# Expert stage of a decoder step: every U group in three passes, with top-k and routing spread over the groups, and the modulated norms in four parts

## The reference, cut to what matters

```python
sh1, sc1, gt1, sh2, sc2, gt2 = split(c @ w_ada + b_ada, 6)
h  = rmsnorm(x, norm1_w) * (1 + sc1) + sh1          # first modulated norm
proj = h @ w_in                                     # attention and delta-rule branches follow
x  = x + gt1 * (mixed @ w_out)
h2 = rmsnorm(x, norm2_w) * (1 + sc2) + sh2          # second modulated norm
qh = h2 @ w_peer_q                                  # 8 heads x 256
s1, s2 = qh[..., :128] . keys[:, 0], qh[..., 128:] . keys[:, 1]    # 8 heads x 2 x 128 scores
v1, i1 = top_k(s1, 16); v2, i2 = top_k(s2, 16)
best, sel = top_k(v1[:, None] + v2[None], 16)       # 16 of 256 pairs a head
wts = softmax(best); eidx = i1 * 128 + i2 at sel    # 128 experts a token, of 16384
act = gelu(h2 . w_peer_u[eidx])
y = x + gt2 * sum(wts * act * w_peer_v[eidx])
```

## Time and profile before

| | |
|---|---|
| median of three runs | 3261.43 us (3259.88 to 3264.95) |
| the profiled execution's own time | 3260.47 us |
| its span, first to last instruction | 3258.7 us |
| PE, PEld busy | 92%, 84% of the span |
| DVE, ACT, Pool busy | 51%, 28%, 23% |
| granted PE clock, mean | 0.952 |

### The profile page before, as it was taken

The page is one execution under the profiler, slowest core; times in us unless marked ns, Lnnn a source line. Parts: engine busy times, 40 slices in busy tenths (PEclk is TensorE's granted clock), DMA queues, the critical chain, the costliest instruction groups (busy, mean ns, idle before and its releaser), DMA issues.

```text
span 3258.7 us, 51780 instructions
## 1 busy us (share of the span) xinstructions
PE 3001.6 (92%) x20823; PEld 2725.9 (84%) x20823; DVE 1676.7 (51%) x2590; ACT 921.3 (28%) x1187; POOL 749.9 (23%) x269
## 2 busy tenths in 40 slices
PE   5799999877787997997999999999999999999999
PEld 2588877556684886997888889999999999999999
DVE  0348616535315003823297765444445776767675
ACT  1011002412111211333201554333333343434341
POOL 0000000000000002442100004544444454545452
PEclk8899999887876998998999999999999999999999
DMA  9577766371203666552444436555555666566663
GB/s 399 230 268 254 252 248 208 96 247 52 84 33 135 246 249 273 208 182 107 168 146 174 160 159 232 205 205 205 204 205 207 234 220 233 220 229 224 222 232 130
DMA packets 144309, 650.46 MB, mean 200 GB/s; under 512 B 22470, under 2 KB 84294, under 8 KB 103110
## 3 DMA queue, kind: packets, MB, share of 16 engines
q1 hardware_dynamic: 134550, 614.26, 50.9%
q10 hardware_dynamic: 9648, 34.61, 2.7%
HBM read 605.12 MB, written 52.07 MB: 202 GB/s over the span
## 4 chain that ended last, share of the span: by engine, by line
PE 82%; DVE 8%; DMA 5%; ACT 2%; issue 1%; SPq 1%; DVEq 1%; ACTq 0%
PE psum L978 16%; PE psum L979 16%; PE psum L980 15%; PE psum L557 15%; PE psum L1060 7%; DMA ring<-in_w_ada 3%; PE psum L537 2%; PE psum L768 1%; PE psum L1087 1%; PE psum L847 1%; PE psum L932 1%; PE psum L949 1%; DVE arena L1704 1%; DMA route_w<-arena 1%; DVE arena L2055 1%
## 5 line engine op out<-in xcount | busy, mean ns | idle before, releaser
L557 PE MATMUL psum<-hT,ring 128*128 128x264 f32 x2560 | 590.6, 393 | 12.6 <-DVE xT L1845 6.6
L979 PE MATMUL psum<-act_hi,w_lo 128*128 128x264 f32 x2048 | 584.9, 286 | 0.0
L557 PEld LDWEIGHTS psum<-hT,ring 128*128 128x128 f32 x2560 | 491.6, 193 | 106.4 <-issue 15.2
L978 PE MATMUL psum<-act_hi,part 128*128 128x264 f32 x1920 | 546.9, 285 | 2.8 <-DVE hT L2124 2.8
L980 PE MATMUL psum<-act_lo,part 128*128 128x264 f32 x1920 | 547.3, 285 | 0.0
L499 POOL TENSOR_TENSOR w_lo<-ring,wd_hi 128x1024 fp32r<-128x1024 f32 x48 | 129.5, 2717 | 1446.9 <-ACT wd_hi L1417 1446.9
L516 POOL TENSOR_TENSOR w_lo<-ring,part 128x1024 fp32r<-128x1024 f32 x112 | 311.7, 2790 | 387.3 <-ACT part L1543 386.0
L979 PE MATMUL psum<-h_hi,w_lo 128*128 128x264 f32 x1376 | 390.3, 284 | 0.0
L979 PEld LDWEIGHTS psum<-act_hi,w_lo 128*128 128x128 f32 x2048 | 386.0, 188 | 0.0
L978 PE MATMUL psum<-h_hi,part 128*128 128x264 f32 x1288 | 366.2, 284 | 2.5 <-issue 2.5
L980 PE MATMUL psum<-h_lo,part 128*128 128x264 f32 x1288 | 365.5, 284 | 0.0
(11 more groups left out here) (421 smaller groups left out, 4592.7 us busy)
## 6 DMA issues: line engine op xcount, KB each, us to landing
ring<-in_w_peer_u SPq DMA_DIRECT2D x64, 2048.0 KB, 8.1
ring<-in_w_peer_v SPq DMA_DIRECT2D x128, 1024.0 KB, 6.9
ring<-in_w_ada SPq DMA_DIRECT2D x48, 2048.0 KB, 11.2
ring<-in_w_in SPq DMA_DIRECT2D x42, 2048.0 KB, 7.9
gelu_scratch<-CK ACTq DMA_DIRECT2D x64, 264.0 KB, 7.8
route_w<-arena ACTq DMA_DIRECT2D x3, 5632.0 KB, 17.6
Wb<-route_w SPq DMA_DIRECT2D x96, 176.0 KB, 3.8
ring<-in_cache_cmp SPq DMA_DIRECT2D x64, 256.0 KB, 4.8
```

The costliest lines, as they stand in the source:

```text
L557: mm = pe.matmul(bank[b + j][:, 0:NT], w[:, k, j * P:(j + 1) * P], hT[:, k, :], start=(k == 0), stop=(k == KT - 1))
L978: pe.matmul(out, w_top, x_top, start=start, stop=False)
L979: pe.matmul(out, w, x_top, start=False, stop=False)
```

## The change

1. The w_ada loads no longer wait for the constants, and come in the order scale, scale, shift, shift (`FIRST_ADA`), so that every four tiles complete four of the 16 feature tiles. PE sums the squares of x before the w_ada loop; ACT's root and DVE's inverse and product with it follow there. `modulate` is cut into four parts of four feature tiles, each run by DVE after its four w_ada tiles, and PE's small product waits part by part.
2. The second norm is cut in the same way; ACT's hi and DVE's rest follow part by part, and dense tile 16 runs its two hi passes part by part and the third pass after them. `hq_hi` and `h2_lo` now stay for all U groups (the second split of h2, L2069, is gone).
3. All 64 U groups are three-pass. Group 0 runs as dense tile 24. The hi of a group has two buffers, `u_even` and `u_odd`: ACT makes the hi of group e+2 (`group_top`) when group e is done. Of the four quarters Pool subtracts three and DVE one (`group_rest`); PE takes the quarters in the order 1, 2, 3, 0 and waits for each.
4. DVE's top-k for a token tile is cut by eight `group_rest` calls; `turn` follows groups 9, 17 and 25. Groups 27 to 59 each take one routing step in their middle.
5. The routing matrix is stored in 11 blocks of 24 tokens (1.5 MB each, two buffers) and not 3 of 88. For a V pair it is read by one transfer of 528 KB in runs of 96 numbers.
6. Buffers move in the arena; the hi buffers of V follow (`v_hi`). The key weights are loaded before the first U tiles.

```diff
+FIRST_ADA = (8, 9, 0, 1)
-N_EARLY = 20
-N_SPLIT = N_GROUP - N_EARLY
+N_TOP = 24
+ROUTE0 = N_TOP + 3
-N_BLOCK, BLOCK = 3, 88
+N_BLOCK, BLOCK = 11, 24
+N_STEP = N_BLOCK * STEPS
...
+        u_even, u_odd = quarters("u_even", arena, 4224, 4), quarters("u_odd", arena, 10496, 2)
+        u_odd = quarters("u_odd_a", adaS, 0, 1) + quarters("u_odd_b", params, 0, 1) + u_odd
+        u_hi = [u_even, u_odd]
...
-            sp.wait_ge(S["consts_in"], 16 * 6)
-
             with sp.Fori(0, N_ADA0 // 4) as i:
                 for s in range(4):
-                    load(s, i, tile_of("w_ada", 4 * i + s))
+                    load(s, i, tile_of("w_ada", 2 * i + FIRST_ADA[s]))
+
+            sp.wait_ge(S["consts_in"], 16 * 6)
...
-            for s in range(2):
-                load(s, U_USE, I["w_peer_u"][s])
-            sp.wait_ge(S["pq_evac"], 8)
+            sp.wait_ge(S["x_summed"], 2)
             sp.dma_start(keys, I["w_keys"]).then_inc(S["keys_in"], 16)
-            for s in (2, 3):
+            for s in range(SLOTS):
                 load(s, U_USE, I["w_peer_u"][s])
...
-                for n in range(N_BLOCK):
-                    sp.dma_start(Wb[:, n].rearrange("p q t -> p (q t)"), route_w[n][:, bass.ds(4 * p, 4), :].rearrange("p q t -> p (q t)")).then_inc(S[f"act_in{b}"], 16)
+                sp.dma_start(Wb[:].rearrange("p n q t -> p n (q t)"), route_w[:, :, bass.ds(4 * p, 4), :].rearrange("n p q t -> p n (q t)")).then_inc(S[f"act_in{b}"], 16)
...
+            def split_rest(s, parity, e):
+
+                for c, n in ((1, 1), (2, 3), (3, 4)):
                     r = slice(c * SLOT // 4, (c + 1) * SLOT // 4)
+                    pool.wait_ge(S["split_hi"], 4 * (e + N_DENSE) + n)
+                    pool.tensor_tensor(w_lo[:, s, r], ring[:, s, r], u_hi[parity][c], ALU.subtract).then_inc(S["split_lo2"], 1)
...
+            for k in range(KT):
+                pe.wait_ge(S["x_squared"], k // 4 + 1)
+                mm = pe.matmul(bank[7][:, 0:NT], ones[:], hT[:, k, :], start=(k == 0), stop=(k == KT - 1))
+            mm.then_inc(S["x_summed"], 1)
             with pe.Fori(0, N_ADA0 // 4) as i:
...
-            pe.wait_ge(S["h_ready"], 1)
             pe.wait_ge(S["wsmall_in"], 16)
             for k in range(KT):
+                if k % 4 == 0:
+                    pe.wait_ge(S["h_ready"], k // 4 + 1)
...
-            pe.wait_ge(S["o_split"], 8)
-            for n in range(8):
-                dense(16 + n, "pq_evac", hq_lo, hq_hi)
+            split_done(16)
+            for k in range(KT):
+                if k % 4 == 0:
+                    pe.wait_ge(S["o_top"], k // 4 + 5)
+                for j in range(2):
+                    w, w_top = dense_tile(16, k, j)
+                    pe.matmul(bank[j][:, 0:NT], w_top, hq_hi[:, k, :], start=(k == 0), stop=False)
+                    pe.matmul(bank[j][:, 0:NT], w, hq_hi[:, k, :], start=False, stop=False)
...
+            def group(s, parity, e, m=None):
+
+                pe.wait_ge(S["gelu_early"], e + 1)
+                for j in range(2):
+                    if j and m is not None:
+                        route(m)
+                    for c in (1, 2, 3, 0):
+                        if j == 0:
+                            if c:
+                                pe.wait_ge(S["split_lo2"], 3 * e + U_SPLIT + c - 3)
+                            else:
+                                pe.wait_ge(S["split_lo"], e + U_SPLIT)
...
+            for e in range(1, ROUTE0):
+                group(e % 4, e % 2, e)
+                if e % 8 == 1 and e > 1:
+                    turn(e // 8 - 1)
+            with pe.Fori(0, N_STEP // 4) as i:
+                for n in range(4):
+                    e = ROUTE0 + n
+                    group(e % 4, e % 2, 4 * i + e, 4 * i + n)
...
+            def group_top(e):
+
+                s = e % 4
+                act.wait_ge(slot_full[s], 16 * (U_USE + e // 4 + 1 - PAGED[s]))
+                if e >= 3:
+                    act.wait_ge(slot_used[(e - 2) % 4], U_USE + (e - 2) // 4 + 2)
+                for c in (1, 0, 2, 3):
+                    r = slice(c * SLOT // 4, (c + 1) * SLOT // 4)
+                    act.activation(u_hi[e % 2][c], ring[:, s, r], ACT.Copy).then_inc(S["split_hi"], 1)
...
+            for e in range(1, N_GROUP - 2):
+                group_top(e + 2)
+                take_gelu(e)
+                if e < N_TOP and e % 8 == 6:
+                    softmax_exp(e // 8)
+                if e < ROUTE0 and e % 8 == 1 and e > 1:
+                    take_chosen(e // 8 - 1)
+                if 0 <= e + 1 - ROUTE0 < N_STEP:
+                    take_route(e + 1 - ROUTE0)
...
+            for k in range(0, KT, 4):
+                rescale(xT, hT, k)
+            for i in range(N_ADA0 // 4):
+                for s in range(4):
+                    ada_bias(4 * i + s, 2 * (2 * i + FIRST_ADA[s]))
+                dve.wait_ge(S["ada_done"], 4 * i + 5)
+                modulate(0, hT, 4 * i)
...
+                best_eight(sc, val, 0, 16)
+                group_rest(e + 1)
+                take_eight(sc, alt, val, idx, range(8))
+                group_rest(e + 2)
+                step(take_eight(sc, alt, val, idx, range(8, 16)))
+                best_eight(alt, val, 8, 16)
+                group_rest(e + 3)
+                index_next(alt, val, idx, 16)
...
+            for m in range(N_STEP):
                 for b in range(2):
 
+                    dve.wait_ge(S["route_mm"], 2 * m + b + 1)
                     for t in range(4):
+                        col = 8 * m + 4 * b + t
+                        dve.tensor_scalar(O2[:, b, t, :], cst("iota"), IT[:, 1, col:col + 1], IT[:, 2, col:col + 1], ALU.is_equal, ALU.mult)
+                        ins = dve.tensor_scalar(O1[:, b, t, :], cst("iota"), IT[:, 0, col:col + 1], None, ALU.is_equal)
                     ins.then_inc(S["onehot"], 1)
+                group_rest(m + ROUTE0 + 1)
```

More of the change, by code:

```diff
@@ L492, in _ @@
             pool.memset(gateS[:], 0.0).then_inc(S["consts_set"], 1)
-            for q in range(N_DENSE):
+            for q in range(N_DENSE + 1):
                 s = q % 4
@@ new lines, in _ @@
+            first_group()
+            pe.wait_ge(S["pq_evac"], 8)
+            pe.wait_ge(S["keys_in"], 16)
+            for a in range(3):
+                scores(a)
+            for e in range(1, ROUTE0):
[6 more added lines that the diff above has]
+                    group(e % 4, e % 2, 4 * i + e, 4 * i + n)
@@ L1137, in pair_values @@
+            for e in range(ROUTE0 + N_STEP - N_STEP % 4, N_GROUP):
+                group(e % 4, e % 2, e, e - ROUTE0 if e < ROUTE0 + N_STEP else None)
             def pair_values(b, p, first=False):
@@ L1606, in windows @@
+            dve.wait_ge(S["h_ready"], 4)
             def windows(src, n):
```

350 lines of the change are left out of this document (136 added, 214 removed).

## The result

The changed kernel takes 3137.69 us, the median of four runs (3124.84, 3151.07, 3130.37, 3145.02), against 3260.65 us for four runs of the kernel before. The ratio is 0.9637 with a 95% interval of 0.9608 to 0.9665; a second measurement of five runs gave 3137.87 and 0.9632 (0.9612 to 0.9653). The forecast was faster, 3158 us within 3145 to 3195: the direction and the mechanisms held, the size did not.

What follows compares the result with a forecast made beforehand. PE was taken to bound the U and V stages. Gains of 23.3 (start), 6 (second norm) and 75 (U), less 2 (V), sum to 102.3 us, giving 3158 us, range 3145 to 3195.

Steps and rivals of the forecast that it cites:

- Bound: U and V stages: both parts of U, and V after them, hang on PE; a three-pass tile takes 11.606 us.
- Start: Up to the small product: norm work runs while w_ada loads arrive, gaining 23.3 us (20.4 to 25.7).
- The 20.4 for the steps that are gone: Start: PE's small product begins at 102.62 and not at 123.00, a gain of 20.4 us.
- the small product: Start: PE's product after the w_ada work, 10.06 us behind a pause, gets 0 to 2.8 us shorter; 1.4 taken.
- The early loads: Start: w_ada loads issued without the wait for the constants gain 0 to 2.5 us; 1.5 taken.
- Second norm: Second norm to the end of dense tile 16: working in four parts gains 6 us (0 to 8).
- U stage: U stage: three-pass groups and waits covered by other groups, less 4 us of new waits, gain 75 us (68 to 79).
- the 2 for the first subtraction: U stage: the first subtraction waits for all three scores and 16 maxima, costing 2 us.
- the 2 for the lock: U stage, top-k: DVE's two-input operations wait for Pool, 9 us for three tiles at worst, none at half the wait.
- rival 1: U stage: DVE waits for Pool in every instruction that reads SBUF; three tiles lose 84 us, time 3238; chance 7%.
- V stage: V stage: the first pair's w_peer_v halves, queued behind the second `Wb`, lose 2 us (0 to 4).
- the lock that the prediction cites: DVE and GpSimd share one port pair, locked per instruction; DVE takes it only with two SBUF inputs or two-port modes.

Runs made afterwards that it cites:

- fp32_groups: Changed kernel with U groups 1 to 19 as one fp32 product each instead of three passes; ratio 0.9801 to the kernel before, 51.4 us over the changed kernel.
- route_quarter: Changed kernel with one token of four in PE's routing products; ratio 0.9525 to the kernel before, U 44.3 us shorter.
- loads_late: Changed kernel with its w_ada loads behind the wait for the constants again; ratio 0.9662 to the kernel before.
- iota_psum: Changed kernel with the row 0 to 127 that routing's one-hot rows are compared with read from PSUM; ratio 0.9644 to the kernel before.
- before_again: The kernel before, without an edit, run later; 3251.80 us over 12 runs.
- after_again: The changed kernel, without an edit, measured again over five runs; ratio 0.9632 to the kernel before.
- start_back: Changed kernel with the start of the kernel before; ratio 0.9730 to the kernel before, 31.3 us over the changed kernel.

## Why the prediction was right in kind and short in size

**Bound: right.** The prediction saw U and V hanging on PE's bare work and priced them by 11.606 a tile and 1.84 a step. U is PE's own work now, as fp32_groups and route_quarter show: 822.4 to 825.6 in the six profiles of kernels with this U stage and no edit to it, where the old one had 898.1 to 904.4 in three.

**Start: right, 1 to 3 us short.** 23.3 predicted, 24.2 to 26.2 by the pieces (133 to 106.9 or 108.6). The 20.4 for the steps that are gone came as summed. The term that was mis-sized is the small product, for which 1.4 of 0 to 2.8 was taken: it gained 2.86. It took 10.0 to 10.2 us in the three profiles with the old start and 7.3 in all others but loads_late, from its first start to its last end. The early loads gave 0.9 to 1.4, near the 1.5 taken. The last w_ada product, which the sum left as it was, took 0.3 to 1.6 us less.

**Second norm: right, 2 to 3 us short.** 6 predicted, 8.0 to 8.7 measured. The new course was priced to 0.3 us (22.1 from the inverse to the end of tile 16, by the prediction's sum; 22.3 measured). Short was the old one: its tile was taken at 11.6 and ended at 1510.6 and not at 1508.6, the slow beginning "up to 2 us" that the prediction named and left out: the tile took 13.6 us at a granted clock of 0.86, after a pause of PE of 16.7.

**U stage: right, -1 to 5 us short.** 75 predicted, 74.0 to 80.3 depending on which execution of the kernel before is the base. Against the execution that the sum was made from, two terms were short: the scores took 16.7 us (1550.47 to 1567.16) and not 20.3, 2 of it the wait for the third score copy and 1.6 a granted clock of 0.90 instead of 0.83; and PE waited for a rest only once, 1.9 and not 4: the 2 for the first subtraction came, the 2 for the lock did not. The reasons for caution were sound: DVE was busy for 82.4 us in the second token tile's groups, 20 more than the 61.8 with a light Pool (62.7 by the prediction's sum), of the 33 that were feared; its idle time of 8 to 18 us a tile was enough. One sign of the prediction failed: "DVE's operations with one input keep their durations." One-hot rows were locked out, about one in each routed group, 71 us of DVE's time in all (264 rows at 546 in place of 275) and none of PE's. So rival 1 is true of these rows, at no price here. The prediction's evidence against it, L2126, reads its other input from PSUM; so do the rows of iota_psum, and they were not locked out either.

**V stage: the loss did not come.** 2 lost predicted, none measured: 760.0 to 762.3 in the 15 profiles with the new stage, 760.9 to 762.7 in the three with the old one. `Wb` landed in 5.1 us, near the estimate of 5.6, but the first pair did not wait for it: PE's wait there, 3.0 us, is for DVE's first rest.

**The sum and its range: these are the steps that failed.** The mechanisms held, and three sizes were wrong.

1. The terms. 102.3 was predicted; the pieces give 116.8 for the first two profiles and 113.2 for before_again and after_again, 10.9 to 14.5 more. That is over the 112.7 that the prediction's own bounds allowed. In these two pairs V makes 4 of it, where 2 lost were taken, U 3 to 5, the norm 2 to 3 and the start 1 to 3.
2. The base. The sum starts from one profiled execution and a median of 3261.4; later measurements of the kernel before have medians of 3251.8 to 3255.6. That is 6 to 10 us, and it lies in the untouched stretch for the most part: 1347.2 in that execution, 1338.6 in before_again. (By its own terms, 3156.4 + 1.77 + 0.96, the sum also gives 3159 and not 3158.)
3. The spread. "The range adds below it the 3 us by which single runs differ": three runs gave this 3. Runs of either kernel spread by 18 to 26 us (3246.92 to 3264.95 before, 3124.84 to 3151.07 after), and the untouched stretch alone is 1328 to 1352 long, shorter where the granted clock is higher while PE works in bursts. The prediction held no term for it.

Terms and base together are 17 to 24 us, and the result lies 20 below the prediction; the pieces of single executions can't split it more finely.

**Not settled.** start_back is 31.3 us slower by the medians, its pieces give 25 to 27. What makes the two passes of bf16 cheap, the weight load or another effect of the type, no run separates. And why the clock falls in one execution and not in the next, with the same instructions, no run here shows.

## What to carry to other kernels

Before a range is set, take the stretches in which PE works in bursts at a granted clock below one: they make executions of the same code differ by more than many a term, and a sum that starts from one execution inherits its luck. When work is spread beside a full engine, count what the helper has idle per group, and count for DVE beside Pool not only operations with two SBUF inputs but also one-input rows from SBUF; reading the constant input from PSUM takes them out of the lock. Where a product has few columns, do not price a pass by its columns: compare one of each type first, the weight load beside it.

## What the runs showed of the hardware

- One-hot rows (TENSOR_SCALAR, one SBUF input, 128 columns) took up to 2.55 us beside a Pool subtraction and 0.27 to 0.35 with Pool's work cut to an eighth; the same rows from PSUM never over 0.42. MAX8, also with one SBUF input, was not touched (277 ns, highest 416). The Trainium skill, "VectorE: DVE Perf Modes", section "Mode 2×_2P — use both read ports for one tensor", states that this mode takes one tensor input, in SBUF, PSUM having a single read port. With the lock that the prediction cites this fits the rows: from PSUM they take 402 ns against 335, and their waits are gone.
- A pass of 128 columns took 111 ns in fp32r and 56 in bf16, with weight loads shown at 192 and 98; one of 264 columns in fp32r took 121.
- The granted clock over the same 905 matrix products was 0.93 in one execution and 0.83 in another, and the stretch was 11.7 us longer.
- In the one execution where the last w_ada tile landed at 97.94 and not at 96.58, the next two pieces of PE's work took 14.5 us in place of 10.25, at granted clocks of 0.50 and 0.77 in place of 1.00.
